# Decode attention reordered, with its value products in four row groups, and the prompt's bias tables built inside it

## The chip, the cores and the metric
The kernel runs on one core of a Trainium2 chip, in one launch. The metric is the device time of that core in microseconds (us), lower is better.

## The reference
One layer of a decoder for two groups of requests that share weights: a prompt of 1,024 tokens and eight sequences that each decode one token on a cache of 2,048. Attention has 8 query heads on 2 key/value groups of width 64 and three branches (compressed blocks, 16 selected blocks of 64 keys, a window of 512 keys). Each branch adds a relative bias that depends on head and distance, has a softmax of its own, and is weighted by a gate:

```python
s = jnp.einsum('bqghd,bcgd->bghqc', qblk, kc) * scale
s = s + table3[_rel_bucket(dist_c)].transpose(2, 3, 0, 1)
p_c = _masked_softmax(s, (dist_c >= 0)[None, None, None])
...
imp = jnp.einsum('bghqc,cs->bgqs', p_c, blk_map)     # importance of each block
...
_, top = lax.top_k(imp, n_top)                       # selected blocks
...
o_nsa = (bg[:, :, 0] * o_c + bg[:, :, 1] * o_s + bg[:, :, 2] * o_w).reshape(B, L, NSA_QW)
```
A recurrence over four heads, a merge, an output projection and a convolutional feed-forward network follow. The change doesn't touch them.

## The kernel before
The kernel is a row of stages; each is a block with a program for every engine, and a barrier of all five engines stands between two blocks. In order: modulation and norm, attention projections, `compress` (which also makes the decode scores on selected blocks, in banks 4 to 7 of PSUM), `decode_attention`, `prompt_attention`, the recurrence's projections, recurrence and merge, output projection, feed-forward. There is no scheduler: each engine runs its program in the written order and waits on semaphores.

`decode_attention` works on 64 rows, 8 sequences by 8 heads. Its steps:

- **Bias.** A 33-row table `tab64` times a one-hot matrix `oh` gives the bias of each row and key, in six pieces `pieces` (L1159); ScalarE copies them to `bias` (L1222). `oh` and six small constants come first on SyncE's queue.
- **First scores.** Queries `Qz` times compressed keys `kcT` (L1162), and the new token's scores and gates (L1163 to L1165), after all six constants (`const_in`).
- **Window.** For each sequence b a load of 256 KB, four transposes (L1173), a copy by ScalarE (L1227), a product (L1177). Each load waits for the one before (`kw_in`).
- **Rank.** From the compressed branch's probabilities TensorE makes the importance of blocks (L1183 to L1187) and VectorE ranks them (L1278 to L1285), masks the scores `S` and takes their minimum (L1290). ScalarE takes the exponentials in the order compressed, window, selected (L1230).
- **Values.** After transposes of the probabilities (L1190 to L1197) each sequence has a chain of 23 products that add up in one [8, 128] piece of PSUM, all at partitions 0 to 7 (L1204 to L1211), 16 of them on the selected values `VS`. `VS` has `VR` = 4 buffers of 1 MB, filled by indirect DMAs from GpSimd (L1148); the fifth waits for the first sequence (`pv_done`). Results go to `oR` (L1316), are transposed (L1215) and land in `oT` (L1320).

`prompt_attention` begins with the bias of the prompt: table times one-hot matrix (L1420), to SBUF (L1568), to the DRAM tensor `bias_rows` (L1380), and back as tables in which row p starts one element later (L1389, L1390). Only then can VectorE score the first step (L1574). 32 steps follow.

Of the kernel before, what the change touches and what calls it, by code (L numbers as in the profile page):

```python
# [16 lines left out]
ALU = mybir.AluOpType  # L17
ACT = mybir.ActivationFunctionType
AX = mybir.AxisListType
# [34 lines left out]
R_TOEP, R_WTOEP = W_TOEP + P - 1, W_WTOEP + P - 1  # L54

# [58 lines left out]
def build(nc, a, o):  # L114
# [21 lines left out]
    with ExitStack() as ctx:  # L136
# [10 lines left out]
        m["x1"] = nc.dram_tensor("x1_rows", [T, D], F32)  # L147

        m["h_hi_dram"], m["h_lo_dram"] = (nc.dram_tensor(x, [P, KD, T], F32) for x in ("h_hi_rows", "h_lo_rows"))
        with ExitStack() as left:  # L150
            with ExitStack() as att:
# [13 lines left out]
                with ExitStack() as dec:  # L165
# [6 lines left out]
                    m["oT"] = sb(left, "oT", [P, 4, T])  # L172
                    decode_attention(nc, a, o, m, PS, sem)
# [894 lines left out]
def decode_attention(nc, a, o, m, PS, sem):  # L1068
# [9 lines left out]
    VR, KR = 4, 2  # L1078
    tab_in, oh_in, const_in, kw_in, vw_in = (sem("da_" + x) for x in ("tab_in", "oh_in", "const_in", "kw_in", "vw_in"))
# [5 lines left out]
    with ExitStack() as st:  # L1085
        def sb(name, shape, dt=F32):
            return st.enter_context(nc.sbuf_tensor(name, shape, dt))
        tab = sb("tab", [NTAB, HEADS])
        tab64 = sb("tab64", [NTAB, R])
        oh = sb("oh_dec", [NTAB, B_NEW + 1])  # L1090
        bias = sb("bias_dec", [R, B_NEW + 1])
# [29 lines left out]
        oR = sb("o_rows_dec", [HEADS, NB * GD])  # L1121
        block = st.enter_context(nc.Block())
        pieces = [(i, min(512, B_NEW + 1 - i)) for i in range(0, B_NEW + 1, 512)]

        @block.sync
        def _(sp):
            sp.dma_start(tab[0:BUCKETS, :], a["rel_table"][:, :]).then_inc(tab_in, 16)
            sp.dma_start(oh[:, :], a["c_oh_dec"][:, :]).then_inc(oh_in, 16)
            sp.dma_start(blkmap[:, :], a["c_blkmap"][:, :]).then_inc(const_in, 16)
            sp.dma_start(same[:, :], a["c_samegroup"][:, :]).then_inc(const_in, 16)  # L1130
            sp.dma_start(seqof[:, :], a["c_seqof"][:, :]).then_inc(const_in, 16)
            sp.dma_start(seqofT[:, :], a["c_seqof_t"][:, :]).then_inc(const_in, 16)
            sp.dma_start(headof[:, :], a["c_headof"][:, :]).then_inc(const_in, 16)
            sp.dma_start(earlier[:, :], a["c_earlier"].to_broadcast([R, NF * NF])).then_inc(const_in, 16)
            for b in range(NB):
                if b >= KR:
                    sp.wait_ge(kwT_done, b - KR + 1)
                sp.dma_start(kw[:, b % KR, :], a["cache_win_k"][0, b].rearrange("(p s) g d -> p (s g d)", s=4)).then_inc(kw_in, 16)
                sp.wait_ge(kw_in, 16 * (b + 1))
            sp.dma_start(vw[:, :, :], a["cache_win_v"][0].rearrange("b (p s) g d -> p b (s g d)", s=4)).then_inc(vw_in, 16)  # L1140

        @block.gpsimd
        def _(pool):
            table = a["cache_sel_v"][0].rearrange("n (c s) g d -> (n c) (s g d)", s=STRIDE)
            for b in range(NB):
                if b >= VR:
                    pool.wait_ge(pv_done, b - VR + 1)
# [4 lines left out]
        def _(pe):  # L1152

            pe.wait_ge(tab_ready, 1)
            pe.wait_ge(oh_in, 16)
            for i, (c0, cols) in enumerate(pieces):
                if i >= 3:
                    pe.wait_ge(bias_read, i - 2)
                pe.matmul(PS[0:R, 1 + i % 3, 0:cols], tab64[:, :], oh[:, c0:c0 + cols], start=True, stop=True).then_inc(bias_mm, 1)  # L1159
            pe.wait_ge(const_in, 16 * 6)  # L1160
            for b in range(NB):
                pe.matmul(PS[0:R, 0, 0:NCD], Qz[:, 64 * b:64 * b + 64], kcT[:, b, :], start=b == 0, stop=b == NB - 1)  # L1162
            pe.matmul(PS[0:R, 0, 128:136], Qd[:, :], ksT[:, L:T], start=True, stop=True)  # L1163
            pe.matmul(PS[0:R, 0, 136:144], Qd[:, :], kwT[:, L:T], start=True, stop=True)
            pe.matmul(PS[0:R, 0, 144:168], seqofT[:, :], bg[0:NB, NT, :], start=True, stop=True).then_inc(first_done, 1)  # L1165

            pe.wait_ge(bias_read, len(pieces))
# [1771 lines left out]
```

## Time and profile before

| | |
|---|---|
| median of 3 runs | 2572.31 us (2566.64 to 2573.69) |
| profiled execution, its own time | 2569.55 us |
| span of the profile (first to last instruction) | 2567.8 us |
| decode_attention in that trace | 549.7 to 661.5 us |
| from there to the first score of prompt_attention | 661.5 to 684.9 us |
| mean granted TensorE clock | 0.946 |

The profile shows one execution; its times are from the span's start. A granted clock of 1.00 is TensorE at 2.4 GHz, 0.50 is 1.2 GHz. PE is TensorE's matmuls, PEld its weight loads, DVE VectorE, ACT ScalarE, POOL GpSimd, SP SyncE.

### The profile page before, as it was taken

To read this page: it belongs to the slowest core of one execution; us is meant where nothing else is said; L and a number is where in the kernel's file an instruction comes from. 1 tells how busy PE (TensorE), PEld (TensorE's weight loads), DVE (VectorE), ACT (ScalarE), POOL (GpSimd) and SP (SyncE) were. 2 spreads that over 40 slices of the span, in tenths; PEclk is the share of its full clock that TensorE was granted. 3 is DMA by queue.
4 is the path that set the end of the run, shared out by engine and by line. 5 is a ranking of instruction groups with operands and counts; after the bars stand their busy time and mean duration, and the time that the engine had idled before them with its cause. 6 is when DMAs were issued, how large, how long until landed. Compare 5 with 4: busy or idle time off the path is not lost. (4 is left out here: it accounts for less than half of the span.)

```text
span 2567.8 us, 34690 instructions
## 1 busy us (share of the span) xinstructions
PE 2300.3 (90%) x14464; PEld 1977.7 (77%) x14464; DVE 960.5 (37%) x1865; ACT 643.8 (25%) x1311; POOL 694.9 (27%) x419
## 2 busy tenths in 40 slices
PE   3996999986788987996789999995999999999997
PEld 2994777853466667996689999443999898998986
DVE  6003343123266661037942024343332323232327
ACT  2102222121256651223431220022221121211213
POOL 3203232010011112113431111153342341423426
PEclk8997999777799999998899999997999999999999
DMA  6536344143300004100022110313120110201112
GB/s 230 177 116 233 124 148 132 41 157 104 136 28 28 1 2 132 50 17 9 19 83 84 33 50 17 139 61 119 47 75 25 50 50 25 75 27 49 56 36 85
DMA packets 136615, 197.07 MB, mean 77 GB/s; under 512 B 15254, under 2 KB 105296, under 8 KB 131730
## 3 DMA queue, kind: packets, MB, share of 16 engines
q1 hardware_dynamic: 128091, 150.74, 18.3%
q0 software_dynamic: 8368, 44.12, 5.0%
q8 instruction: 115, 1.88, 0.3%
q14 instruction: 41, 0.34, 0.0%
HBM read 172.74 MB, written 26.36 MB: 78 GB/s over the span
## 5 line engine op out<-in xcount | busy, mean ns | idle before, releaser
L2629 PE MATMUL PS<-part_hi,w_ff_hi 128*128 128x344 f32 x1056 | 339.8, 322 | 0.0
L2629 PE MATMUL PS<-part_lo,w_ff_hi 128*128 128x344 f32 x1056 | 338.0, 320 | 0.0
L2629 PE MATMUL PS<-part_hi,w_ff_lo 128*128 128x344 f32 x1056 | 338.0, 320 | 0.0
L2629 PEld LDWEIGHTS PS<-part_hi,w_ff_hi 128*128 128x128 f32 x1056 | 199.6, 189 | 6.2 <-issue 5.8
L2629 PEld LDWEIGHTS PS<-part_hi,w_ff_lo 128*128 128x128 f32 x1056 | 199.4, 189 | 0.0
L2629 PEld LDWEIGHTS PS<-part_lo,w_ff_hi 128*128 128x128 f32 x1056 | 199.1, 188 | 0.3
L2751 POOL TENSOR_TENSOR w_ff_lo<-w_raw,w_ff_hi 128x1024 fp32r<-128x1024 f32 x44 | 105.6, 2401 | 302.3 <-ACT w_ff_hi L2702 302.3
L1530 ACT ACTIVATE scores<-scores,mins_p 128x640 f32<-128x640 f32 (+5 forms) x192 | 113.4, 592 | 165.6 <-DVE mins_p L1574 165.6
L2808 DVE TENSOR_SCALAR conv_sb<-up_sb,conv_wT 128x1024 f32<-128x1024 f32 x22 | 41.7, 1896 | 293.9 <-ACT up_dec L2718 293.9
L473 PE MATMUL PS<-h_hi,w_hg_parts 128*128 128x344 f32 x576 | 138.0, 322 | 8.9 <-DMA part_lo<-h_lo_rows 8.9
L2666 PE MATMUL PS<-w_down_hi,act_hi 128*128 128x512 f32 x352 | 139.4, 396 | 0.0
L2666 PE MATMUL PS<-w_down_lo,act_hi 128*128 128x512 f32 x352 | 138.8, 394 | 0.0
L2666 PE MATMUL PS<-w_down_hi,act_lo 128*128 128x512 f32 x352 | 138.6, 394 | 0.0
L1932 PE MATMUL PS<-h_hi,w_merge_parts 128*128 128x344 f32 x768 | 132.0, 324 | 0.0
L2832 DVE TENSOR_TENSOR y_sum<-y_sum,PS 128x512 f32<-128x512 f32 x112 | 76.3, 687 | 138.3 <-PE PS L2666 138.0
L2331 PE MATMUL PS<-w_out_sb,mix 128*128 128x512 f32 (+1 forms) x288 | 127.5, 602 | 0.2 <-DMA w_out_sb<-w_out 0.2
L1932 PEld LDWEIGHTS PS<-h_hi,w_merge_parts 128*128 128x128 f32 x768 | 122.6, 189 | 3.1 <-issue 3.0
L461 POOL TENSOR_TENSOR w_merge_parts<-w_merge_raw,w_merge_parts 128x1024 fp32r<-128x1024 f32 x24 | 59.3, 2493 | 209.5 <-ACT w_merge_parts L454 209.5
L473 PEld LDWEIGHTS PS<-h_hi,w_hg_parts 128*128 128x128 f32 x576 | 100.8, 190 | 9.3 <-DVE lbT L1730 7.7
L2331 PEld LDWEIGHTS PS<-w_out_sb,mix 128*128 128x128 f32 (+1 forms) x288 | 51.8, 182 | 72.3 <-issue 68.8
L2702 ACT ACTIVATE w_ff_hi<-w_raw 128x1024 fp32r<-128x1024 f32 x44 | 46.7, 1062 | 220.9 <-PE PS L2629 211.4
L2746 POOL TENSOR_TENSOR w_down_lo<-w_down_scaled,w_down_hi 128x1024 fp32r<-128x1024 f32 x22 | 52.7, 2394 | 157.3 <-ACT w_down_hi L2697 157.3
(479 smaller groups left out, 4824.8 us busy)
## 6 DMA issues: line engine op xcount, KB each, us to landing
w_or_ada<-w_ada SPq DMA_DIRECT2D x8, 2048.0 KB, 8.0
w_raw<-w_up SPq DMA_DIRECT2D x22, 512.0 KB, 5.0
w_raw<-w_gate SPq DMA_DIRECT2D x22, 512.0 KB, 4.2
w_raw<-w_down SPq DMA_DIRECT2D x22, 512.0 KB, 3.7
w_ada_sb<-w_ada SPq DMA_DIRECT2D x4, 2048.0 KB, 22.5
w_hg_raw<-w_in SPq DMA_DIRECT2D x16, 512.0 KB, 3.6
w_merge_raw<-w_in SPq DMA_DIRECT2D x16, 512.0 KB, 4.0
h_hi_rows<-h_hi SPq DMA_DIRECT2D x1, 4128.0 KB, 15.1
```

Source lines behind the costliest of these rows:

```text
L461: pool.tensor_tensor(r32(self.lo[:, u % 2, k, 0:cols]), self.raw[:, s, :, 0:cols], self.hi[:, u % 2, k, 0:cols], ALU.subtract).then_inc(se ...
L473: last = pe.matmul(out, r32(x), r32(y), start=k + i == 0, stop=k == tiles - 1 and i == 2)
L1530: act.activation(S[:, n % 2, g, c:c + cols], S[:, n % 2, g, c:c + cols], ACT.Exp, bias=mn[:, n % 2, x, g:g + 1], scale=-1.0, accum_out=sm[ ...
L1932: last = pe.matmul(PS[:, e % RING, 0:W3], r32(left), r32(right), start=p == 0 and k == 0, stop=p == 2 and k == KD - 1)
L2331: last = pe.matmul(PS[0:r, 2 * (t % 2) + half, :], mix[:, k, P * t:P * t + r], w[:, k, 512 * half:512 * half + 512], start=k == 0, stop=k ...
L2629: last = pe.matmul(PS[:, e % BANKS, 0:cols], r(wt[:, s, k, :]), r(ht[:, k, t0:t0 + cols]), start=k + i == 0, stop=k == KD - 1 and i == 2)
L2666: last = pe.matmul(PS[:, e % BANKS, :], r(at_[:, f % AR, P * t:P * t + P]), r(wt[:, f % GRP, c]), start=f == fs[0] and i == 0, stop=f == f ...
L2702: act.activation(r(wgh[:, int(kind == "gate"), :, :]), raw[:, n % RAW, :].rearrange("p (k n) -> p k n", k=KD), ACT.Copy).then_inc(hi_done, 1)
L2746: pool.tensor_tensor(r(wdl[:, f % GRP, :]), wds[:, :], wdh[:, f % GRP, :], ALU.subtract).then_inc(lo_done, 1)
L2751: pool.tensor_tensor(r(l_), w, h, ALU.subtract).then_inc(lo_done, 1)
L2808: own(v.tensor_scalar(c, up[:, 0:L], taps[0], taps[3], ALU.mult, ALU.add))
L2832: v.tensor_tensor(d, d, s, ALU.add).then_inc(acc_read, 1)
```

## The change
Three things are joined. The order inside `decode_attention` changes: the near part of the one-hot matrix is loaded first, the far part by ScalarE's queue; the compressed branch's exponential, the importance and the rank run before the window; window loads no longer wait for each other; `VS` has six buffers; the order of exponentials becomes compressed, selected, window. The value products go round four sequences, each with its own quarter of the partitions (0, 32, 64, 96). And the prompt's bias rows, with the tables for its first head pair, are made in `decode_attention`, in a tile at the top of SBUF.

```diff
+                    m["toep"] = nc.alloc_sbuf_tensor_at("toeplitz_0", [P, KV, W_TOEP + W_WTOEP], F32, offset=top)
...
-    VR, KR = 4, 2
+    VR, KR = 6, 2
...
-        pieces = [(i, min(512, B_NEW + 1 - i)) for i in range(0, B_NEW + 1, 512)]
+        pieces = [(B_CMP, NCD + 1), (B_WIN, WIN)] + [(512 * i, 512) for i in range(4)]
         @block.sync
-            sp.dma_start(oh[:, :], a["c_oh_dec"][:, :]).then_inc(oh_in, 16)
+            sp.dma_start(oh[:, B_WIN:], a["c_oh_dec"][:, B_WIN:]).then_inc(near_oh_in, 16)
...
             for b in range(NB):
                 if b >= KR:
                     sp.wait_ge(kwT_done, b - KR + 1)
-                sp.dma_start(kw[:, b % KR, :], a["cache_win_k"][0, b].rearrange("(p s) g d -> p (s g d)", s=4)).then_inc(kw_in, 16)
-                sp.wait_ge(kw_in, 16 * (b + 1))
+                sp.dma_start(kw[:, b % KR, :], a["cache_win_k"][0, b].rearrange("(p s) g d -> p (s g d)", s=4)).then_inc(kw_in[b % KR], 16)
+                if b == KR - 1:
+                    sp.dma_start(blkmap[:, :], a["c_blkmap"][:, :]).then_inc(rank_in, 16)
+                    sp.dma_start(same[:, :], a["c_samegroup"][:, :]).then_inc(rank_in, 16)
+                    sp.dma_start(earlier[:, :], a["c_earlier"].to_broadcast([R, NF * NF])).then_inc(rank_in, 16)
+                    sp.dma_start(oh_p, a["c_oh_prompt"][:, :]).then_inc(oh_p_in, 16)
+            sp.wait_ge(rev_read, len(rev_pieces))
+            sp.dma_start(rev[:, :], revS).then_inc(rev_out, 16)
+            sp.wait_ge(rev_out, 16)
+            for g in range(KV):
+                h = HPG * g
+                sp.dma_start(toep[:, g, 0:W_TOEP], bass.AP(rev, h * NREV, [[1, P], [1, W_TOEP]])).then_inc(toep_in, 16)
+                sp.dma_start(toep[:, g, W_TOEP:], bass.AP(rev, h * NREV + R_TOEP, [[1, P], [1, W_WTOEP]])).then_inc(toep_in, 16)
+            sp.wait_ge(toep_in, 64)
...
         @block.gpsimd
                 if b >= VR:
-                    pool.wait_ge(pv_done, b - VR + 1)
+                    pool.wait_ge(pv_done, 1)
...
         @block.tensor
...
+            for b in range(1, NB):
+                window_keys(b)
+                window_scores(b - 1)
+            window_scores(NB - 1)
+            pe.wait_ge(oh_p_in, 16)
+            pe.wait_ge(kwT_read, NB)
+            for i, (c0, cols) in enumerate(rev_pieces):
+                if i >= 2:
+                    pe.wait_ge(rev_read, i - 1)
+                pe.matmul(PS[0:HEADS, 1 + i % 2, 0:cols], tab[UP, :], oh_p[:, c0:c0 + cols], start=True, stop=True).then_inc(rev_mm, 1)
...
+            def four(x, left, right, start=False, stop=False):
+                for q in range(4):
+                    b = 4 * x + q
+                    last = pe.matmul(PS[32 * q:32 * q + HEADS, 2 + x, 0:GD], left(slice(HEADS * b, HEADS * b + HEADS)), right(b), start=start, stop=stop)
+                return last
...
+            for x in range(2):
+                four(x, lambda c: XnT[:, 0, c], lambda b: kv[0:NB, NT, 3 * GD:4 * GD], start=True)
+                four(x, lambda c: XnT[:, 1, c], lambda b: kv[0:NB, NT, 5 * GD:6 * GD])
+                four(x, lambda c: PcgT[0:NCD, c], lambda b: vc[0:NCD, b, :])
+                for i in range(4):
+                    four(x, lambda c: PTw[:, i, c], lambda b: vw[:, b, P * i:P * i + P])
+                for b in range(4 * x, 4 * x + 4):
+                    pe.wait_ge(v_in[b % VR], 16 * (b // VR + 1))
+                for i in range(16):
+                    last = four(x, lambda c: PT[:, i, c], lambda b: VS[:, b % VR, P * i:P * i + P], stop=i == 15)
+                last.then_inc(pv_done, 1)
 def prompt_attention(nc, a, o, m, PS, sem):
         @block.sync
-            sp.dma_start(oh, a["c_oh_prompt"][:, :]).then_inc(oh_in, 16)
-            sp.wait_ge(rev_read, len(pieces))
-            sp.dma_start(rev[:, :], revS).then_inc(rev_out, 16)
-            sp.wait_ge(rev_out, 16)
-            for j in range(HPG):
+            for j in range(1, HPG):
...
         @block.tensor
-            for n, (c, cols) in enumerate(pieces):
-                pe.matmul(PS[0:HEADS, 4 + n, 0:cols], tab[:, :], oh[:, c:c + cols], start=True, stop=True).then_inc(rev_mm, 1)
```

The engines' programs show how rows move. TensorE at the head of `decode_attention`, before (the bias pieces, then scores, then the window's first keys):

```order
L1159 MATMUL PS<-oh_dec,tab 64x512 [waits da_oh_in,da_tab_ready]
L1159 MATMUL PS<-oh_dec,tab 64x512 x2
L1159 MATMUL PS<-oh_dec,tab 64x512 [waits da_bias_read] x2
L1159 MATMUL PS<-oh_dec,tab 64x128 [waits da_bias_read]
L1162 MATMUL PS<-kcT,Qz 64x127 [waits da_const_in]
L1162 MATMUL PS<-kcT,Qz 64x127 x7
L1163 MATMUL PS<-ksT,Qd 64x8
L1164 MATMUL PS<-kwT,Qd 64x8
L1165 MATMUL PS<-bg,seqof_t 64x24
L1173 MATMUL PS<-ident,kw_raw 128x128 [waits da_kw_in,da_bias_read]
```
and after, down to the second sequence's keys:

```order
L1179 MATMUL PS<-bias_and_oh_dec,tab 64x128 [waits da_near_oh_in,da_tab_ready]
L1197 MATMUL PS<-kcT,Qz 64x127 x8
L1198 MATMUL PS<-ksT,Qd 64x8
L1200 MATMUL PS<-kwT,Qd 64x8 [waits da_small_in]
L1201 MATMUL PS<-bg,seqof_t 64x24
L1179 MATMUL PS<-bias_and_oh_dec,tab 64x512
L1179 MATMUL PS<-bias_and_oh_dec,tab 64x512 [waits da_far_oh_in]
L1179 MATMUL PS<-bias_and_oh_dec,tab 64x512 [waits da_bias_read] x3
L1186 MATMUL PS<-ident,kw_raw 128x128 [waits da_kw_in0,da_bias_read]
L1211 MATMUL PS<-ident,S_cmp 127x64 [waits da_pc_ready,da_rank_in]
L1213 MATMUL PS<-blkmap,PcT 64x32 [waits da_pcT_read]
L1186 MATMUL PS<-ident,kw_raw 128x128 [waits da_kw_in1]
```
One bias piece now stands ahead of the scores, five behind them; the importance (L1211 on) stands ahead of seven of the eight window sequences instead of behind all eight.

ScalarE in the same stage, before (bias copies, window copies, then the three exponentials):

```order
L1222 ACTIVATE bias_dec<-PS 64x512 [waits da_bias_mm] x5
L1222 ACTIVATE bias_dec<-PS 64x128 [waits da_bias_mm]
L1227 ACTIVATE KwT<-PS 128x512 [waits da_kwT_done] x2
L1227 ACTIVATE KwT<-PS 128x512 [waits da_win_done,da_kwT_done] x6
L1230 ACT_TABLE_LOAD
L1230 ACTIVATE S_cmp,sums_dec<-S_cmp,mins_dec 64x127 [waits da_mins]
L1230 ACTIVATE S_win,sums_dec<-S_win,mins_dec 64x513 [waits da_mins]
L1230 ACTIVATE S_sel,sums_dec<-S_sel,mins_dec 64x2049 [waits da_mins]
```
and after:

```order
L1270 ACTIVATE bias_and_oh_dec<-PS 64x128 [waits da_bias_mm]
L1275 ACT_TABLE_LOAD
L1275 ACTIVATE S_cmp,sums_dec<-S_cmp,mins_dec 64x127 [waits da_mins]
L1270 ACTIVATE bias_and_oh_dec<-PS 64x512 [waits da_bias_mm] x5
L1285 ACTIVATE KwT<-PS 128x512 [waits da_kwT_done] x2
L1285 ACTIVATE KwT<-PS 128x512 [waits da_win_done,da_kwT_done] x6
L1288 ACTIVATE toeplitz_3861<-PS 8x512 [waits da_rev_mm] x3
L1288 ACTIVATE toeplitz_3861<-PS 8x382 [waits da_rev_mm]
L1275 ACTIVATE S_sel,sums_dec<-S_sel,mins_dec 64x2049 [waits da_mins]
L1275 ACTIVATE S_win,sums_dec<-S_win,mins_dec 64x513 [waits da_mins]
```
The first exponential moved ahead of everything but one copy; the one of `S_sel` stands behind all window copies and the four new copies of prompt bias rows.

## Rows read from the trace of the kernel before

**Rows 1.** The page: busy us (share of the span) and instructions of each engine
```profile
PE 2300.3 (90%) x14464; PEld 1977.7 (77%) x14464; DVE 960.5 (37%) x1865; ACT 643.8 (25%) x1311; POOL 694.9 (27%) x419
```
**Rows 2.** Windows: start:end and length, busy us (instructions) by engine, clock, DMA
```profile
549.70:572.40 22.70, 14.96 (x41) 8.26 (x42) 1.67 (x12) 3.50 (x7) 3.76 (x4) 0.55 0.70 235
572.40:592.90 20.50, 12.24 (x44) 4.24 (x42) 2.35 (x7) 7.01 (x13) 0.00 (x0) 1.00 0.45 138
592.90:615.50 22.60, 4.28 (x29) 3.26 (x30) 18.21 (x30) 2.10 (x2) 0.00 (x0) 0.50 0.10 38
615.50:620.20 4.70, 4.70 (x22) 2.78 (x23) 0.00 (x0) 0.00 (x0) 0.00 (x0) 0.50 0.00 0
620.20:661.50 41.30, 39.96 (x356) 30.34 (x353) 1.73 (x4) 0.00 (x0) 3.75 (x4) 1.00 0.30 102
661.50:684.90 23.40, 7.28 (x12) 1.39 (x12) 2.80 (x6) 0.00 (x0) 0.57 (x1) 0.57 0.78 286
```
**Rows 3.** Timeline, head and window: start, us, engine, line, operation, [idle before <-releaser]
```profile
554.12 9.19 PE L1159 MATMUL PS<-oh_dec,tab 33*64 33x512 f32 x12 [4.72 <-DMA oh_dec<-c_oh_dec]
...
566.63 3.65 PE L1162 MATMUL PS<-kcT,Qz 128*64 128x127 f32 x16 [3.31 <-DMA earlier<-c_earlier]
...
574.75 0.66 PE L1173 MATMUL PS<-ident,kw_raw 128*128 128x128 f32 x4 [1.00 <-DMA kw_raw<-cache_win_k]
...
575.34 1.07 PE L1177 MATMUL PS<-KwT,Qz 128*64 128x512 f32 x2
...
577.37 0.66 PE L1173 MATMUL PS<-ident,kw_raw 128*128 128x128 f32 x4 [0.95 <-DMA kw_raw<-cache_win_k]
```
**Rows 4.** Timeline, from the importance to the transposes of the probabilities
```profile
592.82 0.44 PE L1183 MATMUL PS<-ident,S_cmp 64*127 64x64 f32 x1 [2.62 <-DVE S_cmp L1268]
...
594.95 1.09 DVE L1278 TENSOR_TENSOR rank_gt<-imp_group 64x900 f32<-64x900 f32 x1
...
607.70 2.01 ACT L1230 ACTIVATE S_sel<-S_sel,mins_dec 64x2049 f32<-64x2049 f32 x1 [15.22 <-DVE mins_dec L1290]
...
611.81 1.97 PE L1196 MATMUL PS<-ident,S_sel 64*128 64x64 f32 x16 [1.67 <-DVE xn_dec L1303]
```
**Rows 5.** Timeline, value products of the second sequence, the stage's end
```profile
624.46 3.48 PEld L1211 LDWEIGHTS PS<-VS,PT_dec 128*8 128x8 f32 x32
624.56 3.66 PE L1211 MATMUL PS<-VS,PT_dec 128*8 128x128 f32 x32
...
659.53 0.68 DVE L1316 COPY o_rows_dec<-PS 8x512 f32<-8x512 f32 x1 [20.17 <-PE PS L1211]
```
**Rows 6.** The tile VS, its weight loads and products: ns min/median/max, first and last start
```profile
L1211 PEld LDWEIGHTS PS<-VS,PT_dec x256: 90/90/137, 618.3 to 659.1; 128*8 128x8 f32 x128
L1211 PE MATMUL PS<-VS,PT_dec x256: 272/273/421, 618.5 to 659.2; 128*8 128x128 f32 x128
```
**Rows 7.** Timeline, the head of prompt_attention
```profile
665.66 6.55 PE L1420 MATMUL PS<-PT,tabp 33*8 33x512 f32 x8 [4.73 <-DMA PT<-c_oh_prompt]
...
672.14 0.80 PE L1436 MATMUL PS<-ksT,qT 64*128 64x128 f32 x4
...
684.91 0.29 DVE L1574 CUSTOM_DVE_ANT_0 scores<-PS,toeplitz 128x128 f32<-128x128 f32 x1 [12.12 <-DMA toeplitz_win<-bias_rows]
```
**Rows 8.** Timeline of the first stage: products at partitions 0, 32, 64, 96
```profile
28.13 1.93 PE L293 MATMUL PS<-w_ada_sb,cT 128*32 128x512 f32 x16
```
**Rows 9.** Timeline in prompt_attention: products at partitions 0 and 64 in turn
```profile
699.89 1.09 PE L1492 MATMUL PS<-PT,kv 128*64 128x128 f32 x16
```
**Rows 10.** Timeline of POOL, issue of the first two gathers of selected values
```profile
550.37 0.94 POOL L1148 DMA_INDIRECT VS<-cache_sel_v,cache_rows  x1 [21.85 <-POOLq L658]
551.61 0.94 POOL L1148 DMA_INDIRECT VS<-cache_sel_v,cache_rows  x1 [0.30 <-issue]
```
**Rows 11.** DMA issues 480 to 720 us (KB, us to landing), and landings of VS alone
```profile
kw_raw<-cache_win_k SPq DMA_DIRECT2D x8, 256.0 KB, 2.6
DMA to landing us min/median/max: 5.3/6.9/13.8
```

More of the change, by code:

```diff
@@ L1152, in _, with bias_piece, window_keys @@
         def _(pe):
-            pe.wait_ge(tab_ready, 1)
-            pe.wait_ge(oh_in, 16)
-            for i, (c0, cols) in enumerate(pieces):
+            def bias_piece(i):
+                c0, cols = pieces[i]
                 if i >= 3:
                     pe.wait_ge(bias_read, i - 2)
[L1159 to L1167, printed above, removed]
-            for b in range(NB):
-                pe.wait_ge(kw_in, 16 * (b + 1))
+                pe.matmul(PS[0:R, 1 + i % 3, 0:cols], tab64, oh[:, c0:c0 + cols], start=True, stop=True).then_inc(bias_mm, 1)
+            def window_keys(b):
+                pe.wait_ge(kw_in[b % KR], 16 * (b // KR + 1))
                 if b >= 2:
@@ L1212, in _ @@
                 last.then_inc(pv_done, 1)
[L1213 to L1215 removed]
+            for x in range(2):
+                pe.wait_ge(rows_read, 4 * (x + 1))
+                last = pe.transpose(PS[:, 7, P * x:P * x + P], oR[:, x, :], ident[:, :])
             last.then_inc(oT_done, 1)
@@ L1219, in _, with bias_piece, exponential @@
         def _(act):
-            for i, (c0, cols) in enumerate(pieces):
+            act.dma_start(oh[:, 0:B_WIN], a["c_oh_dec"][:, 0:B_WIN]).then_inc(far_oh_in, 16)
+            def bias_piece(i):
+                c0, cols = pieces[i]
                 act.wait_ge(bias_mm, i + 1)
                 act.activation(bias[:, c0:c0 + cols], PS[0:R, 1 + i % 3, 0:cols], ACT.Copy).then_inc(bias_read, 1)
+            def exponential(i):
+                t = (SC, S, SW)[i]
+                act.wait_ge(mins, i + 1)
+                act.activation(t[:, :], t[:, :], ACT.Exp, bias=mn[:, i:i + 1], scale=-1.0, accum_out=sm[:, i:i + 1]).then_inc(exps, 1)
+            bias_piece(0)
+            exponential(0)
+            for i in range(1, 6):
+                bias_piece(i)
             for b in range(NB):
@@ L1256, in _ @@
             v.tensor_copy(x3[:, 0, 0:1], mn[:, 0:1]).then_inc(mins, 1)
-            v.wait_ge(win_done, NB)
-            own.then(v.tensor_tensor(SW[:, 0:WIN], PS[0:R, 3, :], bias[:, B_WIN:B_WIN + WIN], ALU.add))
-            v.tensor_reduce(mn[:, 1:2], SW[:, :], AX.X, ALU.min).then_inc(mins, 1)
             v.wait_ge(exps, 1)
@@ L1289, in _ @@
             own.then(v.tensor_tensor(v4, v4, smask[:, :].unsqueeze(1).unsqueeze(3).to_broadcast([R, STRIDE, PAST // SELB, 4]), ALU.add))
-            v.tensor_reduce(mn[:, 2:3], S[:, :], AX.X, ALU.min).then_inc(mins, 1)
+            v.tensor_reduce(mn[:, 1:2], S[:, :], AX.X, ALU.min).then_inc(mins, 1)
+            v.wait_ge(win_done, NB)
+            own(v.tensor_scalar(SC[:, :], SC[:, :], gd[:, 0:1], None, ALU.mult))
+            own.then(v.tensor_tensor(SW[:, 0:WIN], PS[0:R, 3, :], bias[:, B_WIN:B_WIN + WIN], ALU.add))
@@ L1305, in _ @@
+            own(v.tensor_copy(XnT[:, 0, :], PS[0:NB, 6, 0:R]))
+            own.wait()
+            v.tensor_copy(x3[:, 0, 1:2], mn[:, 0:1]).then_inc(pT_read, 1)
+            v.wait_ge(pT_done, 2)
             own(v.tensor_copy(PcgT[0:NCD, :], PS[0:NCD, 1, 256:256 + R]))
```

186 lines of the change are left out of this document (94 added, 92 removed).

## The prediction
> **What bounds the kernel now.** I began with the page: TensorE is busy 90% of the span and no other engine over 37% [rows 1]. That is an average over stages, so I cut the stretch that the change touches into windows [rows 2]. From 549.7 to 684.9 us the core goes through decode attention and the head of prompt attention, 135.2 us, and in only one piece of it (620.2 to 661.5) is TensorE busy without a break. Elsewhere one chain runs while the rest waits. Stages are separated by barriers and nothing after 684.9 is edited in kind, so each microsecond that the first score of prompt attention comes earlier should be a microsecond of the kernel. I read five pieces.
>
> Head: TensorE starts on bias at 554.12, when the whole one-hot matrix is in, and on scores at 566.63, when the last constant has landed; its clock is the lower level [rows 2, 3]. Window: one sequence takes 577.37 - 574.75 = 2.62 us, though its transposes and product are busy 0.66 and 1.07; each load waits for the one before [rows 3]. Rank: from the importance at 592.82 to the exponential at 607.70 VectorE works and TensorE idles [rows 4]. Values: 32 instructions of 128 columns issue in 3.48 us, 109 ns each, at the full clock [rows 5]; there are 8 x 23 x 2 = 368. Prompt head: from 661.5 to 684.91 two trips through DRAM, with VectorE waiting 12.12 us for the last table [rows 2, 7].
>
> **The head, costed.** The near part is 640 of 2,688 columns, so I put the first piece at 553.4 instead of 554.12. Then two instructions of 128 columns, 0.4; the compressed scores, 3.65 [rows 3]; six small instructions at the 0.23 that one of those took, 1.4: 558.9. Five pieces remain, ten instructions of 512 columns. The twelve of before are worth 10.5 such and took 9.19, so 8.7, and 0.7 for the last copy: 568.3. The first keys add 0.9 and the importance to the start of the rank 594.95 - 592.82 = 2.1 [rows 4], which gives 571.3. The order also has this chain wait for three constants that now lie behind two window loads, while six gathers run instead of four. At best that costs nothing. At worst it is 2 MB more at the 235 GB/s of this stretch [rows 2], 8.9 us after 566.6, 6.3 later than 569.2. I take 2, nearer the low end, since the gathers were only a part of that traffic. The rank starts at **573.3** (before 594.95).
>
> **Window, rank and exponentials.** VectorE needs 607.70 - 594.95 = 12.75 as before, so the minimum of the selected scores is ready at 586.0. Beside it TensorE goes through seven sequences. With two loads in flight the step is half of a landing (2.6 [rows 11]) and the transposes (0.66), 1.65, about what TensorE needs itself (0.66 + 1.07 = 1.73 with some overlap). I count two steps at the lower clock at 2.6, five at 1.65 and the last product, 14.6: 587.9. The four bias pieces of the prompt follow: 6.55 at the lower clock [rows 7], half of it at the higher. I take 4.5 plus a copy of 0.6: 593.0. Here the new order has a price. On ScalarE the large exponential stands behind all those copies, so it starts at 593.0 instead of 586.0: 7 us of the rank's gain are lost. From there the old steps hold: 611.81 - 607.70 = 4.1 to the transposes, 615.5 - 611.81 = 3.7 to the products [rows 2, 4]. The window's transposes and copies now come behind and add 1.2 (0.7 of TensorE, 0.5 of VectorE by size). The products start at **602.0** (before 615.5).
>
> **The values.** The count stays 368; what changes is the partitions. The nearest rows are favourable. Sixteen instructions of 512 columns going round partitions 0, 32, 64 and 96 took 1.93 us [rows 8], where one after another at four times 109 ns they would take 7.0. And products at two halves, with the same 128 columns, took 1.09 for sixteen, 55 ns each with the 0.27 of the last one taken off [rows 6, 9]. So the price of one lies between 27 ns (four at a time) and 55 (nothing here issues products faster in a run). I take 27, because the row with four quarters reaches nearly four and the limit of 55 is also just what two halves give. The clock: these products began at the lower level and kept it for 4.7 us [rows 2]. I assume the same: 88 instructions at 53 ns, the other 96 of the first half at 27, in sum 7.3: 609.3. Only then are two gathers issued, 1.24 apart [rows 10], with 6.9 to landing [rows 11]: 0.1 + 1.24 + 6.9 = 8.2, until 617.5. The 56 products that don't need them hide inside. TensorE then idles over 6 us, so again 88 at 53 and 40 at 27, 5.8: 623.3. This wait is new: before, a gather had the time of three sequences. The end is as before, 661.5 - 659.53 = 2.0: 625.3.
>
> A rule speaks against this part. The Trainium skill ("TensorE: Matmul & The Clock Gate", Part 3) says that a weight load overlaps matmuls in flight only if their row groups differ; all these use all 128 rows. In the trace loads were busy 3.48 us and products 3.66 over the same 32 instructions [rows 5], so they overlap and the trace disagrees. What it would do is a rival below.
>
> **The prompt head.** All of it but the first scores is gone: 0.8 of matmuls [rows 7] and 0.6 around them, first score at **626.7**. What moved into the decode stage is under cover: a trip of 684.91 - 672.14 = 12.8 at most from 593.0 on, ready at 606, with the products running until 623. If that cover were gone, it would cost the rest of those 12.8.
>
> **Sum.** 684.9 - 626.7 = 58.2 us. The profiled execution took 2569.55, so 2511.4; the median shown is 2.8 higher, and I say 2512. Bounds: the head from -2 (no wait) to +4.3; bias pieces at the full clock -4.4; window from -1.9 (warm) to +5.7 (all at 2.6, and 2.1 for the last product); prompt bias from -1.2 to +2.1; values from -4.6 (all at 27) to +4.4 (all at 55); gathers -1.6 at their 5.3 minimum [rows 11]. Together -15.7 to +16.5: 2496 to 2528.
>
> **Rivals.** (1) *The quarters don't overlap with 128 columns*, all run at 109 ns: first half 20.1 + 2.3 for the cold start, to 624.4; gathers to 632.6; 128 x 0.109 = 14.0; with 3.4 behind, 650.0, a gain of 34.9: 2535. For it: no row has four quarters with 128 columns. Against: rows 8 and 9 each show half of it [rows 8, 9].
> (2) *Slower*: each product lets the array run dry before the next at another quarter may start, and costs its whole duration, 273 ns [rows 6]: 368 x 0.273 = 100.5 from 602.0, plus 3.4, 705.9, 21 us later than before: 2591. It decides from (684.9 - 3.4 - 602.0) / 368 = 216 ns on. Against it: where the products already go round four quarters, sixteen took 1.93 us [rows 8], far less than even one after another (7.0).
> (3) *Weight loads wait for products in flight*: 90 + 109 = 199 ns [rows 5, 6], 73.2 from 602.0 plus 3.4, 678.6, a gain of 6.3: 2563. The Trainium skill's rule named above says this.
> (4) *The head stalls further*: window loads and constants starve behind six gathers, beyond my 6.3: 2528 to 2550. For it: the last constant already took until 566.63 [rows 3].
> (5) *The stage shrinks and the kernel doesn't*: a later stage waits for something that isn't faster (the 4 MB load issued at the start of prompt attention, say). Same time as before. Against: it has some 280 us.
>
> **How the numbers follow.** My forecast has 0.70, rival 1 0.13, rival 4 0.05, rival 5 0.04, rival 2 0.03, rival 3 0.02, and 0.03 is a gain larger than my low end. The forecast's own range is 2496 to 2528; with rival 1 it reaches 2535 and holds 0.83. Faster by over 0.3% (8 us, about what a measurement of this kernel can tell from no change): 0.70 + 0.13 + 0.05 + 0.03 = 0.91. The same: rivals 5 and 3 (6.3 us is under that bound), 0.06. Slower: 0.03.
>
> **What would show it.** In the profile after: the rank starting near 573 while TensorE does window keys; the large exponential behind four small copies, near 593; 184 products in some 7 us, then a gap of 6 us of TensorE released by a gather; no matmul between the barrier and the prompt's first scores, and the first score within 2 us of it. Wrong would be: products over 100 ns apart; a wait for constants beyond 572; the tables of the prompt landing after the last product; prompt attention's 32 steps taking longer than before.

## The result and the profile after

The changed kernel takes 2513.4 us (median of 4 runs, 2512.13 to 2519.61), the kernel before 2571.12 beside it (4 runs, 2566.64 to 2573.69): a ratio of 0.9782, with a 95% interval from 0.9765 to 0.9799. The profiled execution took 2512.13, its span is 2510.3 against 2567.8. The first score of `prompt_attention` now stands at 630.05 instead of 684.91 [rows 7], 54.9 us earlier; 626.7 was predicted. The other 2.6 us of the span come later: 54.9 is still the difference at 1,060 us, some 56 in the recurrence and 57.4 in the feed-forward, in stages that are the same on both sides. What gives them I did not settle. Of all executions in this document one stands apart, a fourth one of e3 that took 5703.41 us; nothing here explains it, and e3's numbers are of the other three.

The page after, busy us by engine (for [rows 1]): TensorE does 34 us less, though six matmul records fewer are in it; the change didn't take work away, it made the products cheaper.

```profile
PE 2266.3 (90%) x14458; PEld 1953.4 (78%) x14458; DVE 959.3 (38%) x1865; ACT 644.1 (26%) x1315; POOL 695.3 (28%) x419
```

The same stretch in windows (for [rows 2]; start:end and length, busy us and instructions of PE, PEld, DVE, ACT and POOL, granted clock, DMA share, GB/s):

```profile
549.55:572.00 22.45, 11.98 (x38) 6.17 (x38) 3.22 (x18) 5.27 (x10) 5.64 (x6) 0.68 0.88 330
572.00:589.00 17.00, 13.24 (x42) 5.43 (x43) 12.14 (x13) 3.58 (x6) 0.00 (x0) 0.72 0.47 121
589.00:603.70 14.70, 8.48 (x39) 3.77 (x39) 7.38 (x19) 5.53 (x9) 0.00 (x0) 0.71 0.72 234
603.70:611.40 7.70, 7.68 (x188) 5.66 (x192) 0.00 (x0) 0.00 (x0) 0.00 (x0) 0.67 0.09 31
611.40:620.50 9.10, 2.08 (x60) 1.35 (x56) 1.15 (x4) 0.00 (x0) 1.88 (x2) 0.73 0.65 230
620.50:626.80 6.30, 6.24 (x129) 4.86 (x129) 0.00 (x0) 0.00 (x0) 0.00 (x0) 0.58 0.02 5
626.80:630.10 3.30, 1.38 (x6) 0.73 (x6) 1.57 (x7) 0.00 (x0) 0.46 (x1) 0.87 0.00 0
```

In the second window VectorE (12.14, the rank) and TensorE (13.24, the window's keys) work side by side; before they came one after the other. The 184 products of the first half take 7.7 us; all 368 took 46 before [rows 2]. The timeline (start, us, engine, line, operation, idle before and its releaser) has the chain and its two waits for DMA:

```profile
554.43 3.46 PE L1197 MATMUL PS<-kcT,Qz 128*64 128x127 f32 x16
...
554.73 0.30 SPq L1149 DMA_DIRECT2D blkmap<-c_blkmap  x1
...
555.07 13.97 SPq L1150 DMA_DIRECT2D samegroup<-c_samegroup  x1
...
574.99 0.47 PE L1211 MATMUL PS<-ident,S_cmp 64*127 64x64 f32 x1 [8.33 <-DMA earlier<-c_earlier]
...
577.14 1.09 DVE L1336 TENSOR_TENSOR rank_gt<-imp_group 64x900 f32<-64x900 f32 x1
...
591.31 3.38 PE L1226 MATMUL PS<-toeplitz,tab 33*8 33x512 f32 x8
...
595.11 1.99 ACT L1275 ACTIVATE S_sel<-S_sel,mins_dec 64x2049 f32<-64x2049 f32 x1
...
603.72 1.04 PE L1242 MATMUL PS<-kv,XnT 8*8 8x128 f32 x16 [1.64 <-DVE x L1376]
...
611.73 0.94 POOL L1169 DMA_INDIRECT VS<-cache_sel_v,cache_rows  x1 [54.37 <-PE PS L1242]
...
620.56 6.23 PE L1242 MATMUL PS<-VS,PT_dec 128*8 128x128 f32 x128 [7.08 <-DMA VS<-cache_sel_v,cache_rows]
...
630.05 0.29 DVE L1620 CUSTOM_DVE_ANT_0 scores<-PS,toeplitz 128x128 f32<-128x128 f32 x1 [1.12 <-PE PS L1491]
```

The row that I hadn't foreseen is the issue of `samegroup`, a load of 16 KB: SyncE spends 13.97 us on it, `earlier` can be issued only behind it, and TensorE then idles 8.33 for `earlier`. The last row shows that the tables are no longer waited for (before, 12.12 us [rows 7]).

### The profile page after: what moved, and what is told of

Read it like the earlier page. It is cut to its first block and busy times, and to the rows that moved or that the text cites. A ratio compares the mean times of both kernels' runs of the same rounds, so it can differ in the third digit from the quotient of the medians.

```text
span 2510.3 us, 34681 instructions
## 1 busy us (share of the span) xinstructions
PE 2266.3 (90%) x14458; PEld 1953.4 (78%) x14458; DVE 959.3 (38%) x1865; ACT 644.1 (26%) x1315; POOL 695.3 (28%) x419
```

## The experiments

One thing has to be known for all of them. In the traces the decode stage starts between 549.5 and 555.8 us, with the same code ahead of it. So I read each experiment by its distance from the stage's first DMA issue to the first score of `prompt_attention`, as well as by its time:

| kernel | stage starts | first score | distance | against the changed kernel |
|---|---|---|---|---|
| before | 549.71 | 684.91 | 135.20 | +54.7 |
| changed | 549.55 | 630.05 | 80.50 | |
| e1, no quarters | 551.36 | 654.20 | 102.84 | +22.3 |
| e2, tables back | 555.56 | 653.23 | 97.67 | +17.2 |
| e3, quarters alone | 551.74 | 670.21 | 118.47 | +38.0 |
| e4, constants first | 554.98 | 634.80 | 79.82 | -0.7 |
| e5, block map first | 550.24 | 627.46 | 77.22 | -3.3 |
| e6, exponential first | 549.75 | 624.47 | 74.72 | -5.8 |
| e7, eight gathers | 554.96 | 624.36 | 69.40 | -11.1 |
| e8, gathers late | 555.64 | 632.58 | 76.94 | -3.6 |
| e9, e5 + e6 + e7 | 554.55 | 618.36 | 63.81 | -16.7 |
| e10, e9 in another order | 553.13 | 624.20 | 71.07 | -9.4 |
| e11, e9 with the map second | 553.64 | 618.95 | 65.31 | -15.2 |
| e12, e6 + e7 | 555.84 | 624.26 | 68.42 | -12.1 |

Each distance is that of one execution, and it has a scatter of its own. Five of these kernels (e1, e2, e6, e7, e12) have the head of the changed kernel unchanged; from the stage's start to the rank they take 26.3 to 27.3 us, and the changed kernel, in its one trace, 27.6. So a difference of about 1 us is not told from none. Since the changed kernel's trace is the slowest of these six up to there, gains read against it are 0.3 to 1.3 us too large by that, and losses as much too small.

**e1, no quarters.** The changed kernel with each sequence's products at partitions 0 to 7, in a bank of its own.

```diff
-                    last = pe.matmul(PS[32 * q:32 * q + HEADS, 2 + x, 0:GD], ...
+                    last = pe.matmul(PS[0:HEADS, BANK[b], 0:GD], ...
```

> The changed kernel with one thing undone: the 184 value products in the trace's count of each half keep their order round four sequences, but all write partitions 0 to 7, each sequence in a PSUM bank of its own. Theory (quarters of the partitions run side by side, 27 ns a product at the full clock, 109 alone): first half 20.1 us plus about 2 for the cold start instead of 7.7, the 56 products that need no late gather take 6.1 of the gathers' 8.8, the last 128 take 14.0 instead of 6.2; the first score of prompt attention is 21 to 24 us later, the kernel near 2535. Rival (the new order or separate accumulation areas give the overlap, not the partitions): no change, near 2513.

Measured: 2538.72 us (2537.19 to 2543.47), ratio to before 0.9888 [0.9871, 0.9905]; 22.3 us of the distance. Its value products on the timeline:

```profile
614.15 14.14 PE L1244 MATMUL PS<-VS,PT_dec 128*8 128x128 f32 x128
...
637.18 14.13 PE L1244 MATMUL PS<-VS,PT_dec 128*8 128x128 f32 x128 [2.59 <-DMA VS<-cache_sel_v,cache_rows]
```

128 products take 14.14 us, 110 ns each, against 4.64 and 6.23 in the changed kernel. The order of the sequences, going round four of them, is the same here; so the partitions make the difference. The first half takes 23.7 us instead of 7.6 and the products of the second 20.5 instead of 8.3, 28 us together; 4.5 come back because the late gathers are then partly hidden (the wait is 2.59 instead of 7.08), and 1.0 because the products start that much earlier in this execution.

**e2, tables back.** The changed kernel with the prompt's bias made at the head of `prompt_attention` again.

```diff
-            for i, (c0, cols) in enumerate(rev_pieces):
-                pe.matmul(PS[0:HEADS, 1 + i % 2, 0:cols], tab[UP, :], oh_p[:, c0:c0 + cols], ...
 (prompt_attention)
+            for n, (c, cols) in enumerate(pieces):
+                pe.matmul(PS[0:HEADS, 4 + n, 0:cols], tab[:, :], oh[:, c:c + cols], ...
```

> The changed kernel with the prompt's bias rows and tables made at the head of prompt attention again, as before the change. Theory (the tables moved off the path, but their four products and four copies stand in front of the large exponential and cost some 4.7 us there): decode attention ends 4 to 5 us earlier, the head of prompt attention costs 22 more, the kernel is 17 slower, near 2530. Rival (the copies cost nothing, the exponential waits for the window anyway): 22 slower, near 2535.

Measured: 2536.38 us (2533.2 to 2536.79), ratio 0.9869 [0.9852, 0.9885]; 17.2 us of the distance. The wait is back, and the large exponential no longer stands behind the copies of prompt bias:

```profile
595.42 1.99 ACT L1251 ACTIVATE S_sel<-S_sel,mins_dec 64x2049 f32<-64x2049 f32 x1
...
653.23 0.29 DVE L1613 CUSTOM_DVE_ANT_0 scores<-PS,toeplitz 128x128 f32<-128x128 f32 x1 [12.72 <-DMA toeplitz_win<-bias_rows]
```

By its distance the exponential is at 595.42 - 555.56 = 39.86, in the changed kernel at 595.11 - 549.55 = 45.56. So the early tables have a price of 5.7 us inside the decode stage (4.8 without the 0.9 by which the rank starts earlier in this execution) and bring some 23 at the prompt's head, 17.2 in sum.

**e3, quarters alone.** The kernel before with nothing but the value products in four quarters (the diff's `four`, with four buffers).

> The kernel before with only the value products in four quarters of the partitions (four buffers for selected values as before, so four gathers start when the first half is done). Theory: products start at 615.5 as before, the first half takes 7.7, then four gathers of 1 MB one after another, 12 us until the last lands, then 6.2 and 2: decode attention ends near 643.5 instead of 661.5, 18 us faster, near 2553. Rival (gathers are bound by their issue, 1.24 us apart, and land 6.9 after it): 19.5 to 20 faster. Rival (quarters pay only together with the new order and six buffers): no gain.

Measured: 2553.06 us (median of 3, 2549.3 to 2556.5), ratio 0.9937 [0.9913, 0.9962]; 16.7 us less distance than before. All four gathers of the second half are now late:

```profile
619.91 4.69 PE L1204 MATMUL PS<-VS,PT_dec 128*8 128x128 f32 x128
...
628.64 0.94 POOL L1148 DMA_INDIRECT VS<-cache_sel_v,cache_rows  x1 [0.30 <-issue]
...
638.68 5.51 PE L1204 MATMUL PS<-VS,PT_dec 128*8 128x128 f32 x128 [12.01 <-DMA VS<-cache_sel_v,cache_rows]
```

The products are as fast as in the changed kernel, but TensorE idles 12.01 us between the halves. Quarters need buffers to be worth their price: the parts of the change don't simply add. With quarters 16.7 alone and 22.3 beside the rest, the six buffers and the order count in what the quarters bring. No run takes back the new order or the six buffers alone. What is left for them, 54.7 - 22.3 - 17.2 = 15.2 us, is a remainder and not a measurement.

**e4, constants first.** The three rank constants ahead of the window's first two loads.

```diff
+            sp.dma_start(blkmap[:, :], a["c_blkmap"][:, :]).then_inc(rank_in, 16)
+            sp.dma_start(same[:, :], a["c_samegroup"][:, :]).then_inc(rank_in, 16)
+            sp.dma_start(earlier[:, :], a["c_earlier"].to_broadcast([R, NF * NF])).then_inc(rank_in, 16)
             for b in range(NB):
```

> The changed kernel with the three constants of the importance and rank loaded ahead of the first two window loads instead of behind them. In the changed kernel the importance waited 8.3 us for the last of them, to 575.0. Theory A (their place in SyncE's queue is the cause): the importance starts within 2 us of the first keys (near 567 to 568), rank, window and all behind it move by 6 to 7 us, kernel near 2507. Theory B (six gathers ahead fill the DMA engines whatever the place): the importance starts at 573 or later, gain under 2 us.

Measured: 2516.88 us (2513.41 to 2518.68), ratio 0.9792 [0.9776, 0.9809]; -0.7 of distance, which is inside the scatter. The constants' place behind two window loads, which I had named in the prediction, is not what makes TensorE wait:

```profile
558.08 15.10 SPq L1145 DMA_DIRECT2D samegroup<-c_samegroup  x1
```

The issue of `samegroup` took 15.10 us here too. In the kernel before, where the block map was the third load and samegroup the fourth, it had taken 2.72. That gave the next question.

**e5, block map first; e8, gathers late.** Two ways to ask what holds that issue: the place of the block map (127 rows) before it, or the number of gathers in flight.

```diff
 e5
+            sp.dma_start(blkmap[:, :], a["c_blkmap"][:, :]).then_inc(rank_in, 16)
             sp.dma_start(tab[64:64 + BUCKETS, :], a["rel_table"][:, :]).then_inc(tab_in, 16)
 e8 (GpSimd, before the fifth gather)
+                if b == 4:
+                    pool.wait_ge(rank_in, 48)
```

> The changed kernel, with the 127-row block map loaded first on SyncE's queue instead of after the bias vector. In the changed kernel SyncE's issue behind that load (samegroup) took 13.97 us. Theory A: the block map's rows interleave on the DMA engines with the running cache gathers and hold the queue; loaded ahead of them it is gone. Then the samegroup issue takes under 3 us, the importance product starts some 6 to 7 us earlier relative to the stage's start, and the first recurrence score as well: about 2507. Theory B: six gathers in flight fill the DMA engines whatever the order is; then nothing moves by over 1 us: 2513.

> The changed kernel, with the fifth and sixth cache gathers held back until the rank stage's three small loads have landed. Theory A: it is the number of gathers in flight that delays those loads: the importance product then starts 4 to 6 us earlier: about 2508. Theory B: the delay is made by the order of the block map and the first gathers, and holding back two of them does nothing to it: the importance product is where it was, and the time 2513.

Measured: e5 2512.66 us (2508.37 to 2517.82), ratio 0.9786 [0.977, 0.9802]; e8 2514.86 (2513.11 to 2515.35), 0.9787 [0.977, 0.9803]. Neither time tells it from the changed kernel; the traces do. e5:

```profile
550.24 0.25 SPq L1139 DMA_DIRECT2D blkmap<-c_blkmap  x1
...
555.09 0.57 SPq L1150 DMA_DIRECT2D samegroup<-c_samegroup  x1
...
571.83 0.47 PE L1211 MATMUL PS<-ident,S_cmp 64*127 64x64 f32 x1 [0.34 <-DMA earlier<-c_earlier]
```

and e8:

```profile
560.85 10.66 SPq L1150 DMA_DIRECT2D samegroup<-c_samegroup  x1
...
576.25 0.47 PE L1213 MATMUL PS<-ident,S_cmp 64*127 64x64 f32 x1
```

With the map first, issued ahead of the first gather too (550.24 against 550.90), the next issues are short and that of `samegroup` takes 0.57 us although six gathers run: the map's place is the cause of the stall, as theory A of e5 said. The two window loads are not, since e4 has the stall without them ahead and e5 has them ahead without the stall. The importance came 3.9 us earlier (571.83 - 550.24 = 21.6 from the start, against 25.4), not 6 to 7. The wait of 8.33 is down to 0.34, but TensorE is now busy until then: it runs the bias products at the lower clock (0.50 from 555 to 575), since they begin later, and the window ends only 1.9 us earlier. The rest of the 3.3 comes mainly from the first half, whose products then run at a granted clock of 0.91 instead of 0.78. In e8, with four gathers in place of six, the issue still takes 10.66, and the importance is at 576.25 - 555.64 = 20.6, 4.8 earlier. That is the size of e8's theory A, while its theory B is right in that the stall remains. So both seem to count: the map's place makes the stall (0.57 against 10.66 to 15.10), and the gathers bear on its length (10.66 with four, 13.10 to 15.10 with six; one trace has four). Why the map holds the queue the traces don't show. The Trainium skill ("DMA: Bandwidth & Descriptors", section "Why a DMA increments its semaphore by 16 and not by 1", on how many engines a transfer gets) says that a tile of 127 partitions goes to a single DMA engine. That would put all its rows in line with the gathers' packets there, but no run here shows the engines one by one.

**e6, exponential first.** ScalarE takes the large exponential before the four copies of prompt bias.

```diff
+            exponential(1)
             for n, (c0, cols) in enumerate(rev_pieces):
                 ...
-            exponential(1)
             exponential(2)
```

> The changed kernel, with ScalarE's large exponential of the decode probabilities put ahead of its four prompt bias copies. Theory A: the copies, which wait for the four one-hot products of the prompt bias, hold up the exponential (595.11, behind a chain end at 590.8): it then starts 4 to 5 us earlier, transposes and value products 4 us earlier, and the first score 4 us earlier, if the second half's gathers come earlier too: about 2509. Theory B: the second half's rows, which land late, swallow it, and the copies end later: under 1 us at the first score: 2513.

Measured: 2513.4 us (2505.34 to 2514.59), ratio 0.9784 [0.9768, 0.98]; its profiled execution has a span of 2503.6, and its distance is 5.8 us shorter.

```profile
589.25 2.00 ACT L1275 ACTIVATE S_sel<-S_sel,mins_dec 64x2049 f32<-64x2049 f32 x1 [0.41 <-DVE mins_dec L1349]
...
594.57 1.96 PE L1231 MATMUL PS<-ident,S_sel 64*128 64x64 f32 x16 [0.57 <-ACT toeplitz L1289]
...
615.57 5.95 PE L1242 MATMUL PS<-VS,PT_dec 128*8 128x128 f32 x128 [7.23 <-DMA VS<-cache_sel_v,cache_rows]
```

The exponential starts 6.1 us earlier by its distance, the transposes 4.9, since PE's order still has the prompt bias ahead of them. Of each, 0.9 was there at the rank already, ahead of what the edit changes. The wait for the gathers keeps its length (7.23), because it begins with the end of the first half, which moved too. The medians of the times don't show it: the interval of this ratio covers 2509.5 to 2517.7, and three of the four executions took 2513.16 to 2514.59.

**e7, eight gathers.** Sequences 6 and 7 go into two tiles that are dead by then (window keys and their transposes; bias and one-hot), issued once the window's scores are done.

```diff
-                    pool.wait_ge(pv_done, 1)
+                    pool.wait_ge(mins, 3)
...
+        slots = [VS[:, i, :] for i in range(VR)] + [kwk[:, :, :].rearrange("p a n -> p (a n)"), bias_oh[:, 0:STRIDE * GD]]
```

> The changed kernel, with places for all eight value gathers: sequences 6 and 7 go into two tiles that are dead by then, issued once the scores are done and no longer after the first half of the value products. Theory A: the wait of 7.1 us between the halves is only the round trip of the two late gathers (issue 611.73 and 612.98, landed 620.5) and goes; with the second half at 5 to 6 us the first score comes 7 to 9 us earlier: about 2505. Theory B: the two gathers collide with the rank stage's loads or come late anyway; then under 2 us: 2512.

Measured: 2506.36 us (2501.18 to 2506.72), ratio 0.9748 [0.9732, 0.9764]; -11.1 of distance, of which 1.1 is there by the first value product, before the edit can count; the other 10.0 are still more than the 7 to 9 of theory A.

```profile
597.57 0.94 POOL L1170 DMA_INDIRECT kw_and_KwT<-cache_sel_v,cache_rows  x1 [34.80 <-DVE mins_dec L1355]
...
611.07 4.89 PE L1243 MATMUL PS<-VS,PT_dec 128*8 128x128 f32 x128
...
615.89 0.62 PE L1243 MATMUL PS<-kv,XnT 8*8 8x128 f32 x16
```

The second half follows the first without a gap and takes from 615.89 to 621.1, at the full clock (1.00 in that window). In the changed kernel the clock had fallen in the wait and was 0.58 while the second half ran. So beside the wait of 7.08 it is the products of the second half that gain, 5.2 us instead of 8.3.

**e9, e10, e11, e12: together.** e9 has e5, e6 and e7; e12 has e6 and e7 alone; e11 has e9's parts with the map behind the bias table; e10 has e9's parts, both exponentials ahead of the copies, and the transposes of the large probabilities ahead of the prompt bias products:

```diff
 e10 (TensorE)
+                pe.matmul(PS[0:HEADS, 7 * (i % 2), 0:cols], tab[UP, :], oh_p[:, c0:c0 + cols], ...
...
             pe.transpose(PS[0:NB, 6, 0:R], xn[:, 0, :], ident[0:R, 0:R]).then_inc(pT_done, 1)
+            bias_row(0)
+            bias_row(1)
             pe.wait_ge(p_ready, 2)
```

> The changed kernel with the three parts that moved the stage's own times put together: block map first on SyncE's queue (1.9 us at the window's end, relative to the stage's start), large exponential before the four prompt bias copies (4.7 us before the value products, 5.5 at the first score), places for all eight value gathers (11.0 us at the first score). Theory A: they lie one behind another and add but for what they share (both the gathers and the block map move the end of the window's K loads): first score 16 to 18 us earlier relative to the stage's start, time 2494 to 2500. Theory B: with the exponential ahead, the order of the prompt bias products, which PE runs before the transposes, is the bound, so that the block map's part is lost: 15 us, 2498 or more.

> The previous kernel, and both exponentials ahead of the prompt bias copies, with the transposes of the large probabilities ahead of the prompt bias products on PE (these products go to PSUM banks 0 and 7, so that no wait is left between them). Theory A: the prompt bias work sat between the exponential and the transposes (0.57 us of wait and some 1 us of order); it moves beside the vector copies, and the value products start 1 to 3 us earlier than in the previous kernel: 2492 to 2497. Theory B: the vector work between exponential and products sets their start anyway: within 1 us of the previous kernel.

> The combined kernel with the block map loaded second on SyncE's queue, behind the bias table, which landed some 2.3 us later when the map went first. Theory A: the late table is what took back the map's gain (the bias products, and with them the window, began later at half clock): with the map second the table is read within 2 us of its issue, the samegroup issue still takes under 3 us, and the first score comes another 1 to 3 us earlier relative to the stage's start (over 18 us before the changed kernel's). Theory B: the window's own chain of K loads, transposes and products at half clock is the bound; nothing moves by over 1 us.

> The changed kernel with the exponential first and all eight gathers placed, the block map where the changed kernel has it. Theory A: the two parts add (4.7 and 11.0 us, with 0.8 shared): first score 15 to 16.5 us earlier relative to the stage's start, so that the block map's place is worth about 1 us in the combined kernel. Theory B: the block map's 3 us at the rank stage do reach the first score once the exponential is first: then this kernel is 3 us or more behind the combined one at the first score.

| kernel | us (lowest to highest of 5) | ratio to before |
|---|---|---|
| e9 | 2501.66 (2496.37 to 2507.3) | 0.9731 [0.971, 0.9751] |
| e10 | 2503.56 (2501.61 to 2510.92) | 0.9745 [0.9726, 0.9764] |
| e11 | 2501.3 (2500.24 to 2508.87) | 0.9736 [0.9716, 0.9756] |
| e12 | 2503.74 (2501.42 to 2507.33) | 0.9739 [0.9721, 0.9756] |

All four beat both kernels: their intervals lie below that of the changed kernel, 0.9765 to 0.9799 (e10's only just). Among them only the distances tell. e9 has the shortest, 16.7 below the changed kernel, inside theory A's 16 to 18; its median time missed the 2494 to 2500, and its profiled execution started the stage 5 us late. e12 is 4.6 behind e9, 2.7 of them by the first value product, so there theory B holds: the map's place does reach the first score once the exponential is first. In e12 the parts don't add (12.1, where 5.8 + 11.1 would be 16.9).

One reason is a stop of TensorE in front of the second half's 128 products, which the trace puts down to "issue", that is, to nothing that the profile shows. It is not a wait for the last two gathers: they landed at 605.9 and 610.2, and TensorE went on at 617.07. What ended shortly before is a DMA packet of 16 KB of the kind "instruction", at 615.50 (the second line is of the DMA view from 614.5 to 615.6):

```profile
617.07 0.12 PEld L1243 LDWEIGHTS PS<-VS,PT_dec 128*8 128x8 f32 x3 [1.45 <-issue]
...
q8 instruction: 1, 0.02, 5.6%
```

The same order of events is in the other three: the packet ends at 610.01, 614.86 and 610.64 in e9, e10 and e11, and TensorE's weight loads go on 1.4, 1.3 and 1.4 us later (1.6 in e12), after stops of 0.37, 2.82 and 1.26. In e7, where the packet ends at 614.54 and these products start only at 617.4, there is no such stop. So I read it as a wait for the program's own instructions, which were loaded while the prompt's tables were moving. It fits the four traces, but no run tests it.

e11's theory A fell: its distance is 1.5 longer than e9's. The bias table was loaded ahead of the map, but SyncE's next issue was held, and the near one-hot came late:

```profile
554.35 2.13 SPq L1142 DMA_DIRECT2D bias_and_oh_dec<-c_oh_dec  x1
...
562.29 0.65 PE L1180 MATMUL PS<-bias_and_oh_dec,tab 33*64 33x128 f32 x2 [8.96 <-DMA bias_and_oh_dec<-c_oh_dec]
```

What follows the map in the queue came late: here the first bias piece starts 3.3 us later from the stage's start than in e9. But by the first value product only 0.2 us of that are left, so it is not what lengthened the distance. The other 1.3 come in the first half (128 products in 4.96 us instead of 4.55) and in the stop described above (1.26 instead of 0.37). e10 is 7.3 behind e9, and neither of its theories has it:

```profile
596.88 3.58 PE L1226 MATMUL PS<-toeplitz,tab 33*8 33x512 f32 x4
...
600.39 0.47 PE L1237 MATMUL PS<-ident,S_cmp 64*127 64x64 f32 x1
...
601.32 3.14 PE L1226 MATMUL PS<-toeplitz,tab 33*8 33x512 f32 x4
```

Eight instructions of prompt bias took 6.7 us in place of 3.4, because the clock was 0.50 from 596.8 to 604.4, after TensorE had idled 3.61 us for the exponential; and half of them stood ahead of the last transposes. Work that ran at the higher clock behind the window was moved behind an idle stretch and doubled. That gives 3.8 of the 7.3 us, by the first value product. Another 2.3 come up to the second half's 128 products, with the stop of 2.82, and 1.4 in these products, which then ran at a granted clock of 0.69 instead of 1.00; 0.2 come back at the end.

## Why the prediction was right, and where its sizes were off

The forecast of 2512 against 2513.4 rests on the right steps; the terms, each as its length in the chain, predicted and measured:

| step | predicted | measured | off |
|---|---|---|---|
| rank starts | 573.3 | 577.14 | +3.8 |
| from there to the window's last product | 14.6 | 14.2 | -0.4 |
| prompt bias, to the large exponential | 5.1 | 3.8 | -1.3 |
| to the first value product | 9.0 | 8.6 | -0.4 |
| first half | 7.3 | 7.6 | +0.3 |
| gathers, to the second half's own rows | 8.2 | 9.2 | +1.0 |
| 128 products of the second half | 5.8 | 6.2 | +0.4 |
| to the first score | 3.4 | 3.3 | -0.1 |

The sum of the last column is 3.3, which is 630.05 less 626.7. That the time came out within 1.4 us of the forecast is luck in part. The stretch that I costed gave 54.9 us where I had said 58.2; 2.6 more came from later stages, which the prediction had at nothing and which I can't explain. And from 2569.55 - 58.2 = 2511.4, with the 2.8 us between that execution and the median, the sum is 2514.2 and not the 2512 that I wrote.

**The head** was mis-sized. I gave 2 us to constants behind window loads. TensorE waited 8.33 for them; since the bias pieces and the first keys were done at 566.7 instead of 569.2, the rank is 5.8 behind the 571.3 that I had without a wait, inside my bound of 6.3, yet not for my reason. I had named "a wait for constants beyond 572" as a sign of being wrong, and it came: it lasted until 574.99. e4 shows that their place among the window loads is worth nothing that its trace can tell, and e5 that the map's place is the cause. Rival 4, a stall beyond my 6.3, did not come.

**Quarters.** I had 27 ns for a product at the full clock: e7's second half, all at the full clock, has 184 in 5.2 us, 28 ns each. The changed kernel's first half has 128 in 4.64 us at a mixed clock. e1 gives the other end, 110 ns. Here rivals 1 and 2 died: the partitions alone are worth 22.3 us. Rival 3, that weight loads wait for products in flight, died too: in the tile `VS` a load takes 132 ns and a product 396 in the median, and 128 pairs pass in 4.64 us, 36 ns a pair. The Trainium skill ("TensorE: Matmul & The Clock Gate", Part 3) says that a weight load overlaps matmuls in flight only if their row groups differ. All of these use all 128 rows and overlap, so the trace and the page differ.

**The new waits** were predicted in place and size: the exponential behind the copies (e6: the exponential 6.1 and the first score 5.8 us earlier when taken away, 0.9 less each without the scatter at the head; I had said 7 at the exponential) and the gathers between the halves (7.08; e7: 10.0 behind the first product, with the clock). What I hadn't counted is that this wait also lowers the clock for what follows it: it is in my 5.8 for the products, but as a given, not as a cost of the wait.

**The prompt head.** The tables were there in time; e2 has a wait of 12.72 us back. "The stage shrinks and the kernel doesn't" is out: the span is 57.5 shorter.

## What to carry to other kernels

Where several small accumulations run with few output rows, give each its own quarter of the partitions and go round them; count beforehand whether the buffers that feed them are released soon enough, since four times faster products turn a hidden gather into a wait (12.0 us with four buffers, 7.1 with six, none with eight). If the issue behind a small load takes long while large transfers run, as behind the map of 127 rows here, try that load ahead of them, and look at what is then issued right behind it. Whether it is the number of rows that counts, no run shows. And price an idle stretch of TensorE with the lower clock after it.

## What the runs showed of the hardware that was not expected

- The issue of a 16 KB load on SyncE took 10.7 to 15.1 us in each of the eight kernels with the new order and the 127-row block map just ahead of it and gathers running (13.97 in the changed kernel, 15.10 in e4, 10.66 in e8), and 0.57 to 1.10 in the four where the map had gone first or second. In the kernel before, with the map just ahead but both issued within 1.1 us of the stage's start, it took 2.72.
- Products of 128 columns at partitions 0 to 7 take 110 ns each at a granted clock of 1.00 even if each sequence has a bank of its own (e1). In four quarters they take 28 at 1.00 (e7, second half), 36 at 0.78 and 49 at 0.58 (the changed kernel's halves).
- TensorE stopped for 1.3 to 2.8 us in e10, e11 and e12 with no engine and no data to wait for, and went on some 1.4 us after a 16 KB packet of instructions had ended.
- The same code ahead of the stage ends up to 6.3 us apart between executions; I didn't find what does that.
